# A pooling stage split between two engines by halves and blocks, and matmuls of constants at the borders of a norm

## What is computed

```
u = h @ w_in                               # pool_in: 256 x 1024
for each of 4 groups of 256 channels, with windows w = 2, 4, 8, 16:
    p = (trailing mean of u over w positions, fewer at the start) - u
y = (p @ w_group, per group) * scale       # pool_group: 4 times 256 x 256
out = y @ w_out                            # pool_out: 256 x 1024
x = layer_norm(ALPHA * x + out)
```

## Times and the profile before

| | us |
|---|---|
| median of 3 runs | 1671.67 |
| lowest and highest | 1669.38, 1672.41 |
| the profiled execution | 1670.81 |
| its span, first to last instruction | 1668.9 |
| PE busy in it | 1584.6 |
| VectorE, ScalarE, GpSimd busy | 997.2, 770.9, 185.7 |

### The profile page before, as it was taken

How to read it: one execution, slowest core, us unless ns; L and a number is a source line. 1 busy time by engine, 2 the same in 40 slices (tenths; PEclk the granted TensorE clock), 3 DMA queues, 4 the chain that set the end, 5 groups by cost and what they waited for, 6 DMA issues and landing times.

```text
span 1668.9 us, 30136 instructions
## 1 busy us (share of the span) xinstructions
PE 1584.6 (95%) x12512; PEld 1534.6 (92%) x12512; DVE 997.2 (60%) x1278; ACT 770.9 (46%) x1006; POOL 185.7 (11%) x143
## 2 busy tenths in 40 slices
PE   7999999988999999999999879999999997799997
PEld 5999998878989999999989679999899997799997
DVE  5876894345766645655465655555655558565545
ACT  3544555444455534544443545443544444354433
POOL 0100002332110001000022012001200013120001
PEclk9999999989999999999999989999999998899999
DMA  8964763222535555455535325554455543344550
GB/s 316 368 246 165 292 229 124 102 77 102 185 145 179 191 185 177 163 190 176 187 141 189 114 79 200 178 194 181 151 179 187 190 177 127 126 152 176 180 192 32
DMA packets 42153, 289.66 MB, mean 174 GB/s; under 512 B 4843, under 2 KB 7019, under 8 KB 7500
## 3 DMA queue, kind: packets, MB, share of 16 engines
q1 hardware_dynamic: 41244, 284.44, 46.9%
q0 software_dynamic: 816, 3.87, 0.6%
HBM read 285.15 MB, written 3.15 MB: 173 GB/s over the span
## 4 chain that ended last, share of the span: by engine, by line
PE 86%; DVE 6%; ACT 3%; issue 2%; POOL 1%; DMA 1%; SPq 0%; ACTq 0%; POOLq 0%; DVEq 0%
PE banks L601 21%; PE banks L603 21%; PE banks L604 20%; PE banks L702 6%; PE banks L704 6%; PE banks L705 6%; DVE w_lo L1504 2%; ACT w_hi L1104 1%; POOL part L567 1%; PE banks L916 0%; PE banks L733 0%; PE banks L827 0%; DMA raw<-in_panels 0%; PE banks L919 0%; PE banks L826 0%
## 5 line engine op out<-in xcount | busy, mean ns | idle before, releaser
L1504 DVE TENSOR_TENSOR w_lo<-raw,w_hi 128x1024 fp32r<-128x1024 f32 x490 | 614.5, 1263 | 532.1 <-ACT w_hi L1104 526.9
L1104 ACT ACTIVATE w_hi<-raw 128x1024 fp32r<-128x1024 f32 x490 | 515.4, 1057 | 578.7 <-PE banks L604 421.4
L601 PE MATMUL banks<-H,w_lo 128*128 128x256 f32 x1920 | 549.5, 286 | 29.6 <-DVE H L1644 20.1
L603 PE MATMUL banks<-H,w_hi 128*128 128x256 f32 x1920 | 548.3, 286 | 0.0
L604 PE MATMUL banks<-H,w_hi 128*128 128x256 f32 x1920 | 546.6, 285 | 0.0
L601 PEld LDWEIGHTS banks<-H,w_lo 128*128 128x128 f32 x1920 | 368.7, 192 | 32.8 <-issue 32.3
L604 PEld LDWEIGHTS banks<-H,w_hi 128*128 128x128 f32 x1920 | 369.1, 192 | 0.0
L603 PEld LDWEIGHTS banks<-H,w_hi 128*128 128x128 f32 x1920 | 369.1, 192 | 0.0
L603 PE MATMUL banks<-HH,w_hi 128*128 128x256 f32 x960 | 270.8, 282 | 0.0
L601 PE MATMUL banks<-HH,w_lo 128*128 128x256 f32 x960 | 270.6, 282 | 0.0
L604 PE MATMUL banks<-HH,w_hi 128*128 128x256 f32 x960 | 270.1, 281 | 0.0
(11 more groups left out here) (285 smaller groups left out, 1706.5 us busy)
## 6 DMA issues: line engine op xcount, KB each, us to landing
raw<-in_panels SPq DMA_DIRECT2D x269, 1024.0 KB, 4.8
bias_rows<-rev POOLq DMA_DIRECT2D x1, 2048.0 KB, 16.9
XS<-in_x_t SPq DMA_DIRECT2D x1, 1024.0 KB, 6.6
near<-bias_rows POOLq DMA_DIRECT2D x8, 128.0 KB, 2.8
out_t<-XS SPq DMA_DIRECT2D x4, 256.0 KB, 2.6
ws<-in_ws_t POOLq DMA_DIRECT2D x1, 512.0 KB, 9.3
cols<-in_cols SPq DMA_DIRECT2D x1, 180.0 KB, 2.4
wdt<-in_wdt POOLq DMA_DIRECT2D x1, 128.0 KB, 5.9
```

Source lines behind the costliest of these rows:

```text
L601: pe.matmul(acc, w_lo[:, panel_slot, at:at + P], operand[:, kk, 0, :], start=starts and c == chunks[0], stop=False)
L603: pe.matmul(acc, w_hi[:, panel_slot, at:at + P], operand[:, kk, 1, :], start=False, stop=False)
L1104: act.activation(w_hi[:, sl, w], raw[:, r, w], ACT.Copy).then_inc(panel_hi, 1)
L1504: vec.tensor_tensor(w_lo[:, sl, w], raw[:, r, w], w_hi[:, sl, w], ALU.subtract).then_inc(panel_lo, 1)
```

## The change

It has two parts.

*Borders.* Behind `stats`, at every norm but the last (seven borders), PE gets 24 matmuls of constants, `ident_r` with `never`, 256 columns each, into a bank that is free and whose content nobody reads: 6 at once, 7 when `stat_var` is there, 4 behind `stat_root`, 4 behind the first `norm_y` and 3 behind the first `norm_hi`.

*Pooling.* `pu` and `pw` get 8 columns of zeros ahead of each block (two memsets on GpSimd, behind the norm sums of down2), so that the small copies fall away. ScalarE copies the banks to `pu`. GpSimd has no subtraction any more: VectorE does both halves. `pool_group` waits for each half by itself, also for the half of its panel (the groups of its weights are put in that order), ScalarE scales and rounds in one operation per block from the bank to `H`, VectorE subtracts per block from the bank, and `pool_out` takes the blocks as they come, wide windows first (its weights' rows are put in that order).

```
+            def keep_busy(n, bank):
+                for _ in range(n):
+                    pe.matmul(banks[:, bank, 0:T], ident_r[:, :], never[:, :].unsqueeze(1).to_broadcast([P, 2, P]),
+                              start=True, stop=True)
+            def busy_border(stage):
+                k, bank = NORMED.index(stage) + 1, stat_bank(stage) + 3
+                keep_busy(6, bank)
+                pe.wait_ge(S["stat_var"], k + 2)
+                keep_busy(7, bank)
+                pe.wait_ge(S["stat_root"], k + 2)
+                keep_busy(4, bank)
+                pe.wait_ge(S["norm_y"], KD * k + 1)
+                keep_busy(4, bank)
+                pe.wait_ge(S["norm_hi"], KD * k + 1)
+                keep_busy(3, bank)
...
-            pe.wait_ge(panel_lo, 2 * (FIRST_PANEL[s] + 1))
-            pe.wait_ge(taken, FIRST_GROUP[s])
-            for m in (4, 5, 6, 7, 0, 1, 2, 3):
-                if m % 4 == 0:
-                    pe.wait_ge(S["pool_lo_wide" if m else "pool_lo"], 1)
...
-            stage_k8("pool_out", H, operand_of("pool_group", 4))
+            for n in range(2):
+                pe.wait_ge(panel_lo, 2 * POOLED + n + 1)
+                pe.wait_ge(taken, FIRST_GROUP[s] - 1 + n)
+                pe.wait_ge(S["pool_lo"], n + 1)
...
+            def pool_ready(k):
+                n, b = (k - 1) // BANKS, (k - 1) % BANKS
+                if b == BANKS - 1:
+                    pe.wait_ge(taken, FIRST_GROUP[s] + n + 1)
+                else:
+                    pe.wait_ge(S["pool_y_lo"], (BANKS - 1) * n + b + 1)
+            stage_k8("pool_out", H, pool_ready)
...
-            stage("pool_in", nothing)
-            for n, g in enumerate((1, 0)):
-                b = slice(BANKS * g, BANKS * g + BANKS)
-                act.wait_ge(S["pool_f"], n + 1)
-                act.activation(PG[:, b, 0, :], pooled[:, b, :], ACT.Copy).then_inc(S["pool_hi"], 1)
-            stage("pool_group", round_into(H))
+            def pool_kept(n):
+                s, g = INDEX["pool_in"], 1 - n
+                products_done(s, n)
+                act.activation(pu[:, BANKS * g:BANKS * g + BANKS, PAD:], group_banks((FIRST_GROUP[s] + n) % 2), ACT.Copy)\
+                    .then_inc(taken, 1)
+            def pool_scaled(n):
+                act.wait_ge(half_used, 2 * POOLED + n + 1)
+                for b in range(BANKS):
+                    at = COLS["pool_scale"] + BANKS * (1 - n) + b
+                    act.activation(H[:, BANKS * n + b, 0, :], banks[:, pool_bank(n, b), 0:T], ACT.Copy,
+                                   scale=cols[:, at:at + 1]).then_inc(S["pool_y_hi"], 1)
+            split_ahead(2)
+            split_ahead(3, (0,))
+            pool_kept(0)
+            split_ahead(3, (1,))
+            split_ahead(4)
+            pool_rounded(0)
+            split_ahead(5, (0,))
+            pool_kept(1)
+            split_ahead(5, (1,))
+            pool_scaled(0)
+            pool_rounded(1)
+            split_ahead(6, (0,))
+            pool_scaled(1)
+            split_ahead(6, (1,))
...
+            def pool_rest(n):
+                b = slice(BANKS * (1 - n), BANKS * (2 - n))
+                vec.wait_ge(S["pool_hi"], n + 1)
+                vec.tensor_tensor(PG[:, b, 1, :], pooled[:, b, :], PG[:, b, 0, :], ALU.subtract).then_inc(S["pool_lo"], 1)
...
+            split_ahead(2)
+            split_ahead(3, (0,))
+            vec.wait_ge(taken, FIRST_GROUP[INDEX["pool_in"]] + 1)
+            vec.wait_ge(S["pads_clear"], 2)
+            doubled(1, 0)
+            doubled(1, 1)
+            split_ahead(3, (1,))
+            doubled(1, 2)
+            doubled(1, 3)
+            pool_means(0)
+            split_ahead(4, (0,))
+            pool_rest(0)
+            split_ahead(4, (1,))
+            vec.wait_ge(taken, FIRST_GROUP[INDEX["pool_in"]] + 2)
+            doubled(0, 0)
+            doubled(0, 1)
+            pool_means(1)
+            split_ahead(5, (0,))
+            pool_rest(1)
+            pool_scaled(0)
+            split_ahead(5, (1,))
+            pool_scaled(1)
+            split_ahead(6)
```

More of the change, by code:

```diff
@@ L975, in _ @@
             stats(2, False, "out")
+            busy_border("out")
             stage_k8("ff1", H, norm_block(1))
@@ L978, in _ @@
             stats(3, False, "ff2")
+            busy_border("ff2")
             norm = [4]
@@ L1067, in _ @@
             stats(norm[0], True, "att_out")
+            busy_border("att_out")
             norm[0] += 1
@@ L1088, in _ @@
-            last.then_inc(half_used, 2)
-            stage_k8("pool_out", H, operand_of("pool_group", 4))
+            for n in range(2):
[3 more added lines that the diff above has]
+                for b in range(BANKS):
+                    m = BANKS * (1 - n) + b
+                    for k in range(2):
+                        at = (2 * n + b // 2) * CHUNK + k * T + (b % 2) * P
+                        pair = PG[:, m // 2 * 2 + k, :, :]
+                        acc = banks[:, pool_bank(n, b), 0:T]
+                        pe.matmul(acc, w_lo[:, POOLED % SPLIT, at:at + P], pair[:, 0, :], start=k == 0, stop=False)
+                        pe.matmul(acc, w_hi[:, POOLED % SPLIT, at:at + P], pair[:, 1, :], start=False, stop=False)
+                        last = pe.matmul(acc, w_hi[:, POOLED % SPLIT, at:at + P], pair[:, 0, :],
+                                         start=False, stop=k == 1)
+                last.then_inc(half_used, 1)
@@ L1595, in stage_x @@
                 run(vec, INDEX[name], split, take_up)
-            def scale_post(s, g, G):
-                products_done(s, g)
-                for b in range(BANKS):
-                    at = COLS["pool_scale"] + BANKS * g + b
-                    last = vec.tensor_scalar(ev[:, G, b, :], banks[:, BANKS * G + b, 0:T], cols[:, at:at + 1], None,
-                                             ALU.mult)
-                last.then_inc(taken, 1)
-                lo_into(H[:, :, :, :])(s, g, G)
             def centred(stage, m):
@@ L2023, in _, with split_ahead @@
             feed_forward(2, 3)
[L2026 to L2043 removed]
+            def split_ahead(p, halves=(0, 1)):
+                q = FIRST_PANEL[INDEX["pool_in"]] + p
+                split(q, *raw_place(q), halves=halves)
@@ new lines, in doubled @@
+            def doubled(g, w):
+                first, last = max(2 * w, BANKS * g), BANKS * g + BANKS
+                reach = 2 ** w
+                here = pw[:, LEVEL[w] + first - 2 * w:LEVEL[w] + last - 2 * w, :]
+                if w:
+                    there = pw[:, LEVEL[w - 1] + first - 2 * w + 2:LEVEL[w - 1] + last - 2 * w + 2, :]
+                else:
+                    there = pu[:, first:last, :]
+                step(vec.tensor_tensor(here[:, :, PAD:], there[:, :, PAD:], there[:, :, PAD - reach:PAD + T - reach], ALU.add))
@@ L2057, in _, with pool_scaled @@
-            stage("pool_group", scale_post)
+            def pool_rest(n):
+                b = slice(BANKS * (1 - n), BANKS * (2 - n))
+                vec.wait_ge(S["pool_hi"], n + 1)
+                vec.tensor_tensor(PG[:, b, 1, :], pooled[:, b, :], PG[:, b, 0, :], ALU.subtract).then_inc(S["pool_lo"], 1)
+            def pool_scaled(n):
+                for b in range(BANKS):
+                    at = COLS["pool_scale"] + BANKS * (1 - n) + b
+                    vec.wait_ge(S["pool_y_hi"], BANKS * n + b + 1)
+                    vec.scalar_tensor_tensor(H[:, BANKS * n + b, 1, :], banks[:, pool_bank(n, b), 0:T], cols[:, at:at + 1],
+                                             H[:, BANKS * n + b, 0, :], ALU.mult, ALU.subtract)\
+                        .then_inc(taken if b == BANKS - 1 else S["pool_y_lo"], 1)
```

75 lines of the change are left out of this document (32 added, 43 removed).

## The result

| | before | after |
|---|---|---|
| median, us (4 runs each) | 1672.04 | 1653.21 |
| lowest and highest | 1669.38, 1672.52 | 1651.62, 1655.62 |
| the profiled execution | 1670.81 | 1651.66 |
| its span | 1668.9 | 1649.6 |

The ratio is 0.9892, with a 95% interval of 0.9873 to 0.9910: 18.8 us less between the medians, where 15.3 were forecast (1655.5, range 1651.5 to 1661.0). A second measurement of the same kernel gave 0.9913 (0.9897 to 0.9930), which is 14.5 us of 1670.47.

What follows compares the result with a forecast made beforehand. PE, busy 95% of the span, bounds the kernel; time is won only where it stands or runs at half clock. Pooling 10.7 plus borders 4.6 make 15.3 us, from 1670.81 to 1655.5, range 1651.5 to 1661.0.

Steps and rivals of the forecast that it cites:

- Pooling, first half: From pool_in to pool_group's first 24 products: they follow with no stand, so PE's 4.95 us wait on GpSimd's subtraction goes.
- Rival 3: Late hand-over in the pooling: VectorE stands for GpSimd's additions or ScalarE's queue is slower; first half 4.6 us later, 1660.1; 12%.
- Pooling, second half: Between pool_group's halves: PE stands for 4.6 us, starts at 1417.4, and the half clock behind it loses 2.3 us.
- The way out: From pool_group to pool_out: blocks pass singly, the 6.47 us stand goes, and pool_out's last product starts 10.7 us earlier.
- the ends of 9 and 12.5: Pooling's gain range in us: 9 with 1.4 more stand and 2.6 lost to clock, 12.5 with 0.5 lost.
- Borders: Fillers at seven borders keep the clock full; VectorE's norm blocks limit the gain, 4.6 us in sum.
- the price by clock alone: The skill page's price for a throttled stretch, half its length here; the prediction said the trace agrees at out, not down2.
- The term for the other borders: At att_out, down1 and pool_out, with the same VectorE work as down2: 0.5 us together, between 0 and 1.
- The clock fell: Rival at the borders: the clock falls in spite of the fillers, which leave holes; 4.6 us go, 1660.1; 13%.
- PE as the limit: Rival: vector steps don't hold PE; five LayerNorm borders each give 1.45 us more, 7.2 us, 1648.3; 4%.
- Slower: Rival at the borders: fillers don't follow each other; at 0.390 us spacing seven borders cost 42 us, 1702; 3%.

Runs made afterwards that it cites:

- Experiment 8: The changed kernel with GpSimd's eight additions of the LayerNorm bias behind down2 working on one token instead of 256: 1654.82 us in one run.
- experiment 6: The changed kernel with 35 more fillers on PE between the halves of pool_group: 1650.46 us, ratio 0.9880 to the kernel before.
- experiment 2: The changed kernel without the fillers at the borders, so the pooling part alone: 1659.26 us, ratio 0.9938 to the kernel before.
- experiment 5: The changed kernel with 48 fillers at each border instead of 24: 1660.19 us, ratio 0.9931 to the kernel before.
- experiment 10: The changed kernel with PE waiting ahead of pool_out until both halves are scaled, rounded and subtracted: 1655.23 us in one run.
- experiment 3: The changed kernel with VectorE's two splits in the norm moved to ahead of the 6th and 8th block: 1648.70 us, ratio 0.9882 to the kernel before.
- experiment 1: The kernel before with the fillers at the seven borders and the pooling as it was: 1662.26 us against 1668.99, ratio 0.9964.
- experiment 7: The kernel before, unchanged, measured again for a second profile: 1669.27 us, ratio 0.9998.
- experiment 9: The changed kernel, unchanged, measured again for a second profile: 1655.42 us, ratio 0.9913 to the kernel before.
- Experiment 12: The changed kernel with later splits, fillers between pool_group's halves and ScalarE's Silu table load behind the seventh rounding: 1646.33 us, ratio 0.9845 to the kernel before.

## Why the prediction was right, and what it missed

**Pooling, first half.** The mechanism held. ScalarE's copy, the doublings and the rounding came in the forecast order, but VectorE was ready 0.7 us later than worked out, and the stand forecast as none was 0.35. I had weighed GpSimd's additions against VectorE's doublings from one row of before and added nothing. Experiment 8 shows that they cost 0.04 to 0.18 us on each operation, 0.36 on the doublings and the split and 0.33 on the means. The Trainium skill's page "SBUF — State Buffer", section "SBUF: two separate sides", describes an exclusive lock between the two engines, in which one blocks fully. The trace of before agrees more than the one row that I weighed. In order of time these are an addition that began ahead of VectorE's split, and the next, beside two splits; a split beside the additions (1.22 is usual); VectorE's copy of 128x4 by itself; GpSimd's subtraction, and the same kind of copy beside it:

```profile
1395.01 0.93 POOL L587 TENSOR_SCALAR XS<-XS,cols 128x256 f32<-128x256 f32 x1 [16.85 <-DVE H L1644]
...
1395.91 2.53 POOL L587 TENSOR_SCALAR XS<-XS,cols 128x256 f32<-128x256 f32 x1
...
1397.65 1.41 DVE L1504 TENSOR_TENSOR w_lo<-raw,w_hi 128x1024 fp32r<-128x1024 f32 x1
...
1402.26 0.17 DVE L2035 COPY pw<-pu 128x4 f32<-128x4 f32 x1
...
1412.24 2.68 POOL L579 TENSOR_TENSOR PG<-pooled,PG 128x1024 fp32r<-128x1024 f32 x1 [4.93 <-ACT PG L1477]
...
1413.89 1.06 DVE L2035 COPY pw<-pu 128x4 f32<-128x4 f32 x1
```

The second copy ends at 1414.95, 0.03 us behind the subtraction: VectorE stood 0.9 us for GpSimd. And an addition that comes first takes 0.93 us, so the mean of 1.54 holds GpSimd's own waits for VectorE. Beside the additions it is mostly GpSimd that stands, and PE does not wait for it there; VectorE lost 0.7 us in all. Rival 3's price of three waits of 1.54 us was too high, and adding nothing was too low.

**Pooling, second half.** PE's stand was forecast at 4.6 us and was 4.12, ending 0.3 us later than worked out; half of that is the late first half, by experiment 8. ScalarE's four scalings took 1.57 instead of 2.0, so its queue held nobody up. The half clock cost 2.4 (forecast 2.3), as experiment 6 shows by removing it. That it came within 0.1 owes something to luck: behind the same stand it was 1.5 in experiments 2 and 5.

**The way out.** No stand ahead of pool_out, as forecast; experiment 10 shows that it would be 2.26 us, and 1.6 of clock. The last product of pool_out stands 10.1 us earlier, counted from the last sum of down2, and the whole stretch is 10.2 us shorter, against 10.7. What is missing in the last product is the start 0.3 us late, 0.1 of clock and 0.25 of pace in pool_out (0.1200), the last again chance. This pair of profiles had the long episodes of half clock on both sides; with a short one on one side the gain is 8.9 or 11.2, at or inside the ends of 9 and 12.5.

**Borders.** Forecast 1.86 at out, 1.04 at ff2, 1.17 at down0, none at down2, 0.5 for the other three. The stretches give 1.77, 0.98 and 1.09, and -0.07 and 0.23 at att_out and down1; down2 lies in the pooling's stretch, with its 49th product at 7.17 after 7.16, and at pool_out the 49th came at 7.16 instead of 7.27. The step that decided it, that VectorE's fifth rest and not the clock holds the 49th product, was right, and experiment 3 shows it by moving VectorE's splits. The first product of the next stage was expected 0.1 to 0.2 us later by the waits of the portions; at down2 it is 4.01 us behind the last sum, as before. The prediction's remark that the trace agrees at out with the price by clock alone is not right, though. There the clock was 0.50 for all of this stretch of before:

```profile
478.30:484.00 5.70, 5.70 (x27) 5.70 (x28) 5.19 (x10) 2.76 (x5) 0.00 (x0) 0.50 0.01 3
```

Half of 5.70 is 2.85, and 1.77 came back: at out, too, PE at full clock waits for VectorE (a stand of 0.30 us at the 25th product, the 49th 6.53 us behind the first, where experiment 5 has 5.70). The sum did not use that price. The term for the other borders was sized on one execution, though. In the three profiles without fillers the 49th product at these seven borders is late by 4.5, 5.1 and 5.3 us in sum against the kernels with them; the rows gave the lowest. The fillers also take away a spread, which one profile can't show.

**The rivals.** The clock fell nowhere behind a border with 24 fillers. PE as the limit (1648.3) is refuted by down2. The late hand-over in the pooling happened to a tenth of its price. Slower was wrong for this number of fillers and is right for twice as many (experiment 5).

**What was not in the sum.** 3.0 us up to the border of out and 2.1 behind pool_out, by which the profiled pair differs from a like pair. Experiments 1, 7, 8 and 9 show both as chance of an execution. What the prediction can claim is the 14.2 us of the stretches, against its 15.3; that 15.3 lies between 14.5 and 18.8 is in part luck. That the medians of 4 runs also differed by 18.8 and not by 14 to 15 is within what such runs do, by the second measurement of the same kernel. I can't exclude that a microsecond of it is real.

## What to carry to other kernels

Ahead of pricing half clock at a stage's start, look at the engine that feeds the stage: where each block waits for it, half clock costs only what remains ahead of the tightest block, and moving a split away from that engine's chain can be worth as much as the clock: 3.7 us on top of the fillers here, against some 4 for the fillers. Whether it is worth that without them was not tried. Fillers in a stand must fit the stand: a third of their number gave the same time here, twice their number cost 5.4 us in the stretches. Compare executions stretch by stretch between marks that both kernels have, so that chance elsewhere isn't credited to the change, and take more than one profile of each: behind the same stand the half clock lasted for 12 products in one profile here and for 25 in another.

## What was not expected of the hardware

Matmuls of 128x256 behind each other, at a granted clock of 1.00, run at one of two paces, and stay with it for a whole stage or longer: 0.1187 us or 0.1200 from start to start. Twenty microseconds of gu3, before and after (length, PE, PEld, DVE, ACT, POOL, PEclk, DMA):

```profile
1480.00:1500.00 20.00, 20.00 (x169) 20.00 (x168) 11.64 (x12) 8.96 (x10) 4.74 (x4) 1.00 0.64 233
```

```profile
1480.00:1500.00 20.00, 20.00 (x171) 20.00 (x170) 11.16 (x11) 9.49 (x12) 0.00 (x0) 1.00 0.55 195
```

169 matmuls are counted in the one and 171 in the other, at the same clock. Over the 1584 products of gu3 and down3 it is 2.1 us. The slower pace was seen behind pool_out in the first profile of before and in experiment 1, behind ff2 in the second profile of before, and in pool_out itself in the changed kernel, but not in its second profile. Experiment 12 has it in pool_out without any half clock ahead of it. What sets it stays open; no run here was made for it.
